# Norm weights turned on TensorE, and the first row tiles of u multiplied one by one, in a hybrid decoder layer

## The reference

```
h = x * rsqrt(mean(x * x) + 1e-6) * norm1_g      # 576 x 1024
z = h @ w_in                                     # u is the first 512 columns of z
u, q, kvc, kvs, kvw, g_nsa, g_a, g_b = split(z)
y_ssm, state = s5_scan(u, state_ssm, lam, log_dt, b, c, d)
```

## Time and profile before

| | us |
|---|---|
| median of 3 runs | 971.21 (970.72 to 972.89) |
| profiled execution, its own time | 972.58 |
| its span | 970.9 |
| PE busy | 882.1 (91%) |
| PEld, DVE busy | 593.8, 352.6 |
| ACT, POOL busy | 185.2, 163.5 |
| mean granted TensorE clock | 0.954 of full |

### The profile page before, as it was taken

One profiled execution on the slowest core, in us unless ns is written; L12 is line 12 of the kernel. 1 busy time (PEld: TensorE's weight loads), 2 busy tenths in 40 slices (PEclk: granted clock), 3 DMA queues, 4 the chain that ended last, 5 costly groups with the idle time before them and its releaser, 6 DMA issues.

```text
span 970.9 us, 11907 instructions
## 1 busy us (share of the span) xinstructions
PE 882.1 (91%) x4183; PEld 593.8 (61%) x4183; DVE 352.6 (36%) x948; ACT 185.2 (19%) x464; POOL 163.5 (17%) x172
## 2 busy tenths in 40 slices
PE   3999999999998979999989999996899999995994
PEld 2455678777786955445757744554677777762441
DVE  3069602555613246663653311324111111113332
ACT  2010213211122324444200000120111111111221
POOL 2049004000030113342000000104211111104100
PEclk9999999999998978999989999988899999997997
DMA  8530763505126490002032091171699999945101
GB/s 261 136 104 0 192 246 115 51 13 167 46 72 141 158 259 18 2 1 93 6 102 75 23 306 65 65 271 44 206 370 333 353 347 347 339 147 195 44 23 54
DMA packets 116079, 140.51 MB, mean 145 GB/s; under 512 B 39170, under 2 KB 95538, under 8 KB 115914
## 3 DMA queue, kind: packets, MB, share of 16 engines
q1 hardware_dynamic: 93084, 110.17, 36.0%
q0 software_dynamic: 5072, 15.52, 4.4%
q10 hardware_dynamic: 17878, 14.21, 4.4%
HBM read 118.65 MB, written 23.33 MB: 146 GB/s over the span
## 4 chain that ended last, share of the span: by engine, by line
PE 85%; DVE 4%; DMA 3%; ACT 3%; issue 2%; another core or an unknown queue 1%; POOL 0%; ACTq 0%; POOLq 0%; DVEq 0%
PE ps L993 67%; PE ps L1247 3%; PE ps L1211 2%; PE ps L1000 2%; PE ps L1233 2%; DMA g_cols<-in_norm_g 1%; PE ps L1396 1%; ACT kvct L1521 1%; PE ps L1114 1%; PE ps L1108 1%; PE ps L1014 1%; DMA kernel_taps<-raw 1%; PE ps L1205 1%; DMA wgu<-expert_rows,pos_i 1%
## 5 line engine op out<-in xcount | busy, mean ns | idle before, releaser
L993 PE MATMUL ps<-hT,w_slot 128*128 128x288 f32 x640 | 155.7, 406 | 0.2 <-ACT fin L1601 0.2
L993 PEld LDWEIGHTS ps<-hT,w_slot 128*128 128x128 f32 x640 | 121.5, 190 | 34.3 <-issue 0.9
L993 PE MATMUL ps<-w_slot,hT 128*128 128x512 f32 (+1 forms) x320 | 129.3, 565 | 0.8 <-ACT hT L1521 0.8
L993 PE MATMUL ps<-wgu,hT 128*128 128x256 f32 x512 | 116.1, 386 | 1.5 <-issue 0.9
L993 PEld LDWEIGHTS ps<-wgu,hT 128*128 128x128 f32 x512 | 98.0, 194 | 15.2 <-issue 1.2
L993 PEld LDWEIGHTS ps<-w_slot,hT 128*128 128x128 f32 x320 | 61.4, 194 | 64.0 <-issue 46.0
L993 PE MATMUL ps<-merged,actT 128*128 128x512 f32 x128 | 59.0, 604 | 8.4 <-PE ps L1396 6.9
L2223 DVE SCALAR_TENSOR_TENSOR th<-th,ps 128x256 f32<-128x256 f32 x16 | 6.7, 421 | 162.7 <-ACT th L1720 162.7
L993 PE MATMUL ps<-w_slot,merged 128*128 128x512 f32 x128 | 55.5, 593 | 1.1 <-DVE merged L1787 1.1
L993 PEld LDWEIGHTS ps<-merged,actT 128*128 128x128 f32 x128 | 23.1, 190 | 34.9 <-issue 34.8
L993 PEld LDWEIGHTS ps<-w_slot,merged 128*128 128x128 f32 x128 | 24.1, 190 | 30.7 <-issue 29.2
(11 more groups left out here) (377 smaller groups left out, 1172.7 us busy)
## 6 DMA issues: line engine op xcount, KB each, us to landing
wgu<-in_w_exp_gate SPq DMA_DIRECT2D x16, 1024.0 KB, 6.7
wgu<-in_w_exp_up SPq DMA_DIRECT2D x16, 1024.0 KB, 9.2
merged<-in_w_exp_down SPq DMA_DIRECT2D x16, 1024.0 KB, 9.0
w_slot<-in_w_in SPq DMA_DIRECT2D x8, 1024.0 KB, 6.7
expert_rows<-onsaT ACTq DMA_DIRECT2D x16, 512.0 KB, 7.4
hT<-gates_by_features SPq DMA_DIRECT2D x8, 576.0 KB, 3.7
w_slot<-in_w_o SPq DMA_DIRECT2D x2, 2048.0 KB, 14.4
w_slot<-in_w_ple_gate SPq DMA_DIRECT2D x2, 2048.0 KB, 16.2
```

What stands on the lines that cost most here:

```text
L993: ins = pe.matmul(out, a, b, start=(n == 0), stop=(n == len(pairs) - 1))
```

## The change

The norm weights are loaded as rows: tile g_rows has 16 partitions of 128 elements, 8 for each weight, so that a piece is 512 bytes. TensorE turns it in one transpose under a new first key ("gains",), and VectorE copies the result to g_cols. The load of the u weights is issued behind the first row tile and ahead of the other four. The plan, TensorE and VectorE take each row tile through all its steps before the next: the plan's order is gains, then for each t the two hT keys and the u key; TensorE turns tile t and multiplies it by u at once; VectorE scales tile t and takes its turned halves. ScalarE's program is unchanged behind the two loads.

```diff
 def make_plan():
     p = Plan()
+    p.add(("gains",), "dve")
     for t in range(NT):
         for k in range(2):
             p.add(("hT", t, k), "dve")
-    for t in range(NT):
         p.add(("u", t), "act")
...
+        g_rows = sb("g_rows", [2 * KD, P])
...
-            for t in range(NT):
+            rows((xp, xs), 0, x_in).then_inc(x_ld[0], 16)
+            load_weights("u")
+            for t in range(1, NT):
                 rows((xp, xs), t, x_in).then_inc(x_ld[t], 16)
-            for name in ("u", "kv0", "kv1"):
+            for name in ("kv0", "kv1"):
                 load_weights(name)
...
             pe.wait_ge(consts, 1)
+            pe.wait_ge(gains_ld, 32)
+            finish(pe.transpose(begin(("gains",))[:, 0:2 * KD], g_rows[:], ident[0:2 * KD, 0:2 * KD]))
             for t in range(NT):
                 p = TILES[t]
                 pe.wait_ge(hn_made, t + 1)
...
                     finish(ins)
-            for t in range(NT):
-                p = TILES[t]
                 o = begin(("u", t))
                 pe.wait_ge(*emptied(("hT", t, 1)))
                 pe.wait_ge(*w_need["u"])
...
-            act.dma_start(g_cols[:, 0], col(I["norm1_g"][0], KD), allow_slow_non_contiguous=True).then_inc(gains_ld, 16)
-            act.dma_start(g_cols[:, 1], col(I["norm2_g"][0], KD), allow_slow_non_contiguous=True).then_inc(gains_ld, 16)
+            act.dma_start(g_rows[0:KD], I["norm1_g"][0].rearrange("(k p) -> k p", p=P)).then_inc(gains_ld, 16)
+            act.dma_start(g_rows[KD:2 * KD], I["norm2_g"][0].rearrange("(k p) -> k p", p=P)).then_inc(gains_ld, 16)
...
-            dve.wait_ge(gains_ld, 32)
+            o = take(("gains",))
+            empty(dve.tensor_copy(g_cols[:].rearrange("p w k -> p (w k)"), o[:, 0:2 * KD]))
+            dve.wait_ge(*emptied(("gains",)))
             for t in range(NT):
                 p = TILES[t]
                 dve.wait_ge(rstd_done, t + 1)
                 dve.tensor_scalar(x_in[0:p, t], x_in[0:p, t], stat[0:p, 2, t:t + 1], None, ALU.mult).then_inc(hn_made, 1)
-            for t in range(NT):
                 turned_norm(dve, t, ("hT", t), 0, take, empty)
```

## The result

The changed kernel's median is 984.92 us (4 runs, 983.85 to 988.26) against 970.97 for the kernel before in the same series; the ratio is 1.0150, 95% interval 1.0125 to 1.0174. It is slower by 14.0 us. The forecast was 985.5, in a range of 981 to 990. The profiled execution took 985.13 us, its span is 983.5.

The account below looks back on a forecast made before the run. TensorE bounds the kernel, so the last u product's end decides. ScalarE free at 44.6, then copy, products and half clock give 68.7 against 54.3, +14.4 us: forecast 985.5 us, range 981 to 990.

Parts of the forecast that it names:

- The place: TensorE before u tile 2: waits some 15 us from about 29 for u tile 0's bank, until ScalarE's load issues end.
- ScalarE free at 44.6: End of ScalarE's parameter load issues: 43.97 before, plus 1.6 for a later start, minus 1.0; bounds 42.1 to 48.9.
- clearing the way for ldt: ACT queue: removing g_cols and weights beside ldt saves at most 1 us, 99 packets per us against 90.
- From there: From ScalarE free to the last u product: copy, u2, tiles 3 and 4; ends at 68.7 against 54.3, +14.4 us.
- the half clock: u tile 2 after TensorE's wait: runs partly at 1.2 instead of 2.4 GHz, costing 2.5 us (1.7 to 3.4).
- tile 3's turn: Before u tile 3: half of the transposes, 0.7 us, then two DVE multiplications of 0.67, in all 2.1 us.
- Rigid shift: After the u products: TensorE is busy from 55 to 150 us, so everything later moves by the same amount.
- A: Rival: ldt is slow only beside other packets; u products end at 58.1, +3.8 us, 975.0 us; 9%.
- B: Rival: with g_cols gone no ScalarE load issue blocks; u products end at 51.4, -2.9 us, 968.3 us; 6%.
- C: Rival: no change in time, ScalarE free at 28.3 to 32.1; 2%.
- The point at which the sign would turn: ScalarE free at about 30.2, 54.3 less the 24.1 us from there to the end, separates faster from slower.
- I took 0: Before the first row tile's scaling: added row loads, transpose, DVE copy and wait were priced at 0 us.

Follow-up runs that it names:

- x1: Changed kernel with log_dt loaded as 128 pieces of 128 bytes instead of 2048 of four; ratio 0.9975 to the kernel before.
- x2: Changed kernel with all S5 parameter loads issued by SyncE behind the kv weights instead of by ScalarE; ratio 0.9976 to the kernel before.
- x3: Changed kernel with u tiles 0 and 1 copied out of PSUM by VectorE instead of ScalarE; ratio 1.0018 to the kernel before.
- x8: Changed kernel with the two ldt loads issued a second time, into a tile nothing reads; 1003.23 us, ratio 1.0346 to the kernel before.
- x7: Kernel before with log_dt loaded as 128 pieces and nothing else changed; ratio 1.0002 to the kernel before.
- x6: Changed kernel with log_dt as 128 pieces and each tile turned one product ahead; 965.18 us, ratio 0.9954 to the kernel before.
- x9: x6 plus 26 identity transposes before u tile 0 and ScalarE's copy of that tile ahead of its load issues; 968.51 us, ratio 0.9908.
- x5: Changed kernel with the old order, all tiles turned, then all multiplied, u weights still ahead of row tiles 1 to 4; ratio 1.0029.
- x4: Kernel before with only the norm weights loaded as rows and transposed, the rest of the change left out; ratio 0.9973.
- x10: x6 with log_dt loaded in four-byte pieces again; 988.94 us, ratio 1.0144 to the kernel before.

## Why the prediction was right, point by point

**The place.** It said that TensorE would wait before u tile 2 for the bank of u tile 0, some 15 us from about 29, and that the page table's issue would end that wait. It waited 14.48 us from 30.6; it asked 1.3 us later than forecast (29.3), since the u weights landed at 10.6 and not 9.6, and that cost nothing, because ScalarE was free much later. Shown by x1, x2, x3 and x8.

**ScalarE free at 44.6.** It was at 44.4, but by two errors that cancel. The last row tile was taken to land at 14.2 and was ready at 16.24 (3.57 and 12.67 in the chain); the load issues began at 17.50, 3.7 us later than before, not 1.6. From 1.6 us that is 14.6 us, where 4.46 MB at 401 GB/s would need 11.1, and I had allowed 1.5 more. The rate was that of a full stretch in the middle: from 1.6 to 16.2 us the mean was 348 GB/s, and 5.09 MB moved in that time, so kv weights were among them already. The bytes account for 1.6 us of the difference, the rate for 1.9. And clearing the way for ldt was priced at 1.0 us, from 99 packets per us against 90; it ran at 108 and the whole run of issues took 26.9 us instead of 30.2, 3.3 less. Errors of + 2.1 and - 2.3: that ScalarE's time came out so well is luck.

**From there.** The copy, 0.65; u tile 2 in 10.0 us, so 2.9 for the half clock and not 2.5; 1.9 for tile 3's turn (2.1), 7.1 for u tile 3 (6.9), 1.3 (1.4) and 3.67 (3.6). The end was 69.04 against 68.7. No step of the mechanism failed; these are the sizes that were off.

**Rigid shift.** The chain of both kernels in order of time, first the kernel before, then the changed one:

```profile
103.84 46.77 PE ps L993 x192
...
606.20 8.56 PE ps L993 x32
...
900.23 13.74 PE ps L993 x32
```

```profile
118.56 46.77 PE ps L996 x192
...
621.28 8.56 PE ps L996 x32
...
912.77 13.73 PE ps L996 x32
```

+14.7, +15.1, +12.5 us. The distance moves by a microsecond or two where one kernel has a stretch at half clock and the other has none or a shorter one: the one at 154.5 us before has no counterpart 14 us later. The two profiled executions thus differ by 12.6, the medians by 14.0. The + or - 1 us that I gave these stretches was a little narrow, and that 985.5 lies within 0.6 of the median is partly luck.

**The rivals.** A (ldt slow only beside other packets) fell on the first look: 1078 packets in 10 us alone on the DMA engines. B (no block with g_cols gone) fell too, and C with it: lam_r was blocked for 4.80 us and the second b load for 14.82. The point at which the sign would turn, ScalarE free at 30.2, was reckoned with 2.5 us of half clock that B leaves out; without them it is 32.7.

**A wrong reading that did no harm.** The prediction sets ldt against g_cols, which "went at 833 per us". That is one picked microsecond, 3.5 to 4.5, of a burst of 1013 pieces in the 2 us from 3. Behind it g_cols slowed down too. Its queue in the kernel before, 5 to 10 and 10 to 15 us:

```profile
q10 hardware_dynamic: 560, 0.00, 7.2%
...
q10 hardware_dynamic: 507, 0.00, 8.0%
```

That is 107 per us, beside the row tiles, whose queue filled the DMA engines (95.0 and 99.1%). The forecast took ldt's own speed and so came out; rival A was priced on the burst alone. The Trainium skill (DMA: Bandwidth & Descriptors, Why small descriptors are slow) gives a small packet a fixed cost of about three cycles and 32 bytes of descriptors. The traces don't speak against that, as the prediction has it: 7 ns of an engine's time for a piece of ldt, 8.8 for one of g_cols in the burst (833 pieces, 45.6% of 16 engines for 1 us). What doesn't follow from it is that ldt would race: the engines were idle for most of the time, and what set the pace is not shown.

**Small points.** The rows of the norm weights landed at 6.3 us, later than the first row tile's sum of squares was ready, and VectorE waited for the transpose (6.64) before it scaled at 6.85. I took 0; it costs some tenths, which the wait for the u weights until 10.6 covers.

## What to carry to other kernels

An engine that both issues loads and frees PSUM banks is a shared resource: before one moves work so that a bank comes round sooner, find in that engine's timeline when it is really free, since the profile can put such idle time down to the producer, as with the 30.27 us before. A block in a queue that costs nothing today (x7) may be the whole price of the next change (x1, and x8 one for one). And an improvement of several parts is best tried part by part: here the first part alone gave 4.7 us in the trace, and the whole lost 14.7. With log_dt in larger pieces the whole gave 2.1, and with the better order too 5.7 (x6; 4.5 by its ratio).

## What the runs showed of the hardware

**A broadcast load in four-byte pieces is slow while the DMA engines idle.** ldt's 2048 pieces ran at 90 packets per us beside the kv weights and at 108 alone, when each took 7 ns of a DMA engine's time and the engines were busy for 4.7%. What spaces them out is not shown. They all read the same few addresses for 64 partitions; that this is the cause was not tried, and g_cols, with another address for each piece, doesn't settle it: it ran at 833 in its burst and at 107 beside the row tiles, and no run has it alone for longer. 128 pieces of 128 bytes with the same content took the block away (x1).

**Transposes raise TensorE's clock.** In x9 TensorE did nothing but 35 transposes until 10.39, and u tile 0 then ran in 7.10 us, as the later tiles do, where it took 10.02 in x6 behind nine. The kernel before agrees: idle until 16.25, it ran 40 transposes in 6.80 us and then four tiles in 27.66, 6.9 each. The Trainium skill (TensorE: Matmul & The Clock Gate, Part 4: PE-mode transpose) says that a transpose doesn't count as busy in the same way and that the full clock doesn't engage for it. Here something did engage: the same product went at twice the rate from its first matmul on. The trace calls these transposes MATMUL and doesn't show whether they ran in the mode that the skill means. The busy times from 10.6 to 13.9 us, first x6, then x9, show 4 matmul records against 8 in the same time, the ratio of the two levels (1.2 and 2.4 GHz). The clock column reads 1.00 in both and doesn't show it, so the level is read from the rate.

```profile
10.60:13.90 3.30, 3.28 (x4) 1.50 (x5) 0.00 (x0) 2.02 (x3) 0.75 (x2) 1.00 1.04 405
```

```profile
10.60:13.90 3.30, 3.30 (x8) 1.39 (x8) 0.21 (x1) 2.26 (x4) 0.75 (x2) 1.00 1.04 397
```

**A wait near 680 us has two lengths.** GpSimd waits for its last scatter of row_of_slot and then loads idx. First the changed kernel, then x1, in order of time:

```profile
696.02 0.60 POOL L950 DMA_DIRECT2D idx<-row_of_slot  x1 [2.16 <-issue]
```

```profile
685.70 0.60 POOL L950 DMA_DIRECT2D idx<-row_of_slot  x1 [7.10 <-issue]
```

The idle time before the load is 2.16 or 7.10 us, in kernels that differ in nothing near it: 2.2 in both kernels of the result and in x5 to x8, 6.9 to 7.3 in x1 to x4 and in x9 and x10. So it goes with the group that was timed together, and the three groups of experiments ran on three chips. The kernel before ran at a median of 975.8 and 976.1 us in the two groups with the long wait, and at 971.0 and 969.8 in the two with the short one. Whether the chip or something else in a group decides it stays open.

The long wait isn't lost whole. Behind it the load lands sooner (the next wait is 1.95 us in x1 and 5.15 before), and from the last scatter to the first gather it is 11.3 us in x1 against 9.6. More is lost further on: x1 is 1.7 us ahead of the kernel before at 604 us and 2.8 behind it at 903, x4 4.7 ahead and 2.4 behind. These compare with a profile of the kernel before that has the short wait; none with the long one was taken. The ratios are taken within a group. In x1, x2 and x9 they agree with the traces (2.4, 2.3 and 8.9 us against 2.1, 2.0 and 8.9); x4's is lower than its trace (2.6 against 4.7), but its interval holds both; x3's is 1.7 us slower where its trace is 2.0 ahead, and why is open.
